# First projections of the recurrence in another order: query thirds ahead of the sample's third of the forget gate

## The chip, the cores and the metric

The kernel runs on one core of one Trainium2 chip, as one launch. The metric is the device time of that core in microseconds (us). The kernel before was timed in 3 runs: median 1388.84 us, lowest 1388.37, highest 1389.0.

## What is computed

One inference step of a two-layer encoder for two request groups that share weights: a prompt of 1024 tokens and a sample of 32 tokens. Layer 0 is sparse grouped-query attention; layer 1 is a gated linear recurrence (8 heads, keys and values of 128). Between them stands a residual add and an RMS norm. The change lies at the border of the two layers. The part of the reference that matters:

```
h = h + attn_out                                   # layer 0 ends
hn = rmsnorm(h, norm_w[1])                         # layer 1 begins
p = hn @ w_in                                      # 1024 -> 4096 columns
q, fp, vi, z = split_cols(p, [REC_KW, REC_KW, REC_WIDTH, REC_WIDTH])
f = lb + (1.0 - lb) * jax.nn.sigmoid(fp)           # forget gate
q = jax.nn.silu(q)
g = jnp.log(f)
k = 1.0 - f
# per head: b = cumsum(g); decays exp(b_t - b_s); scores, outputs and states from q, k, v and the decays
```

## The kernel before, in words

**Tokens and tiles.** The 1056 tokens are 9 tiles: tiles 0 to 7 are the prompt's, 128 tokens each, tile 8 (`SAMPLE`) holds the sample's 32. Layer 1 wants the normed tokens with the model dimension on the partitions. So TensorE (PE) turns each tile with 8 transposes in two groups of four (`turn`, L1310 to L1320), and VectorE (DVE) splits the turned values into a high and a low part (`hn_hi`, `hn_lo`; `split_normed`, L177 and L180), two groups a tile. The sample's normed rows can be made only after its own output product, its residual add, its squares (ScalarE, ACT) and its mean and root (GpSimd, POOL).

**Projections.** Each head has 4 weight tiles of 1024 x 128 (forget, query, value, gate, in this order), and each is multiplied with all tokens in three thirds of 352 tokens (`project(i)`, i = 3 x weight tile + third; 24 matmuls each: L190). Third 0 needs tiles 0 to 2, third 1 tiles 0 to 5, third 2 all of them, the sample's too. A result lies in one of four PSUM banks, taken in turn: bank `(i + 2) % 4`. ACT reads it (`read_projection`, L1731) with Sigmoid for the forget gate, Silu for query and gate, a copy for the value, and the read frees the bank for the projection four places later. The semaphores count places: `acc_ready` the finished projections, `acc_read` the read ones. The first four places wait instead for the last reads of the attention's output product (`out_read`).

**Order around the change.** Every engine's order is written out by hand. PE: output products of tiles 0 to 8, with the turn of tile t - 1 behind the products of tile t; then `project(0)`, `project(1)`, turn of the sample, `project(2)`, and in the loop over heads `project(3)` onwards, with transposes and small products (L1654 k_T, L1658 v_T, L1663 state, L1671 pairs) between. DVE: the splits of tile 7 and of the sample, then the recurrence's constants, whose first instruction (L1891) raises `lb_done`. ACT: the sample's squares, then a wait for `lb_done` and a small Exp (L1742), then the reads of the forget gate's three thirds, the logarithm (L1754), the cast of the next weight tile (L1406) and the query's three thirds. A change of function from Sigmoid to Silu, Ln or Exp puts an ACT_TABLE_LOAD ahead.

**Behind the forget gate.** When all three thirds are read, DVE makes the forget gate (`forget`, L1967 and L1970), after the logarithm a scan (L1926), the differences for the decays (L1929 to L1946: 16 instructions, and between those from L1929 on no semaphore wait), and, when ACT has taken their exponentials (`decay`, L1760), products with the query (`scale_queries`, L1951 to L1963). POOL makes the products with the key (L1839 to L1852), and between them the low parts of the weights (L1413). Then DVE does the next head's `forget` and `carry` (L1984 to L1992), for which PE waits with its pairs.

**Weights.** SyncE (SP) loads a weight tile into one of 3 slots when the last third of the tile that held the slot is done (L1596).

```
            project(0)
            project(1)
            S["turn_sample"](pe)
            project(2)
```

Of the kernel before, what the change touches and what calls it, by code (L numbers as in the profile page):

```python
# [31 lines left out]
SAMPLE = NT - 1  # L32
CW = T // 3
# [151 lines left out]
def product(pe, out, left, right):  # L185

    passes = [(l, r) for k in range(KT) for l, r in ((left[0](k), right[0](k)), (left[0](k), right[1](k)),
                                                     (left[1](k), right[0](k)))]
    for n, (l, r) in enumerate(passes):
        last = pe.matmul(out, l, r, start=n == 0, stop=n == len(passes) - 1)  # L190
    return last
# [1051 lines left out]
def attention_out(nc, S):  # L1243

    io, sem, ps, wide = S["io"], S["sem"], S["ps"], S["wide"]
    stats, half, gT, ident = S["stats"], S["half"], S["gT"], S["ident"]
    w_lo_done, x_in = S["wo_lo_done"], [sem("x2_in0"), sem("x2_in1")]
    g_hi_done, g_lo_done, shifted = sem("g_hi_done"), sem("g_lo_done"), sem("sample_rows")
    added = sem("sample_added")
    out_ready, h_ready, squares_ready = sem("out_ready"), sem("h_ready"), sem("sq1")  # L1250
    mean_ready, rstd_ready, hn_scaled = sem("mean1"), sem("rstd1"), sem("hn_scaled")
    tr_ready, hi_done, lo_done, stored = sem("tr1"), sem("hn_hi1"), sem("hn_lo1"), [sem("h_stored0"), sem("h_stored1")]
# [12 lines left out]
    if True:  # L1265
# [28 lines left out]
        def tensor(pe):  # L1294
            for t in range(NT):
                pe.wait_ge(g_lo_done, t + 1)
                for n in range(2):
                    u = 2 * t + n
                    if u == 0:
                        continue  # L1300
                    if u >= 4:
                        pe.wait_ge(h_ready, u - 3)
                    if u == 1:
                        pe.wait_ge(w_lo_done, 4)
                    output_product(pe, S, (g_hi, g_lo), (w_hi, w_lo), t, n,
                                   range(KT - 1 if u == 2 else 0, KT)).then_inc(out_ready, 1)
                if t >= 1:
                    turn(pe, t - 1)

        def turn(pe, t):  # L1310

            r = rows(t)
            pe.wait_ge(hn_scaled, t + 1)
            for g in range(2):
                if t >= 1:
                    pe.wait_ge(lo_done, 2 * (t - 1) + g + 1)
                for k in range(4):
                    kk = 4 * g + k
                    last = pe.transpose(wide[:, g, k * P:k * P + r], hn[0:r, kk * P:kk * P + P], ident[0:r, 0:r])
                last.then_inc(tr_ready, 1)  # L1320
# [68 lines left out]
                norm_stats_pool(pool, stats, half, t, squares_ready, t + 1, mean_ready, rstd_ready, rows(t))  # L1389

    S["early_out"], S["split_gated_hi"], S["split_gated_lo"] = early_out, split_gated_hi, split_gated_lo
    S["turn_sample"], S["hn_lo1"], S["out_read"], S["sample_read"] = lambda pe: turn(pe, SAMPLE), lo_done, h_ready, shifted
    S["h_stored"], S["out_done"] = stored, out_ready
    return dict(sync=sync, tensor=tensor, scalar=scalar, gpsimd=gpsimd, vector=vector)

# [21 lines left out]
def recurrence(nc, S):  # L1417
# [11 lines left out]
    SLOTS = REC_SLOTS  # L1429


    PER_HEAD = 12
# [35 lines left out]
    by_act = [u[0] in ("k_T", "v_T", "out") for u in products]  # L1468
    n_act = [sum(by_act[:i]) for i in range(len(products) + 1)]
    n_dve = [i - n for i, n in enumerate(n_act)]  # L1470

    def states_done(head):

# [117 lines left out]
    if True:  # L1591
        def sync(sp):
            def load(c):
                if c >= SLOTS:
                    sp.wait_ge(acc_ready, 3 * (c - SLOTS + 1))
                sp.dma_start(raw[:, c % SLOTS], rec_weights(io, c)).then_inc(raw_in[c % SLOTS], 16)  # L1596

            sp.wait_ge(S["out_done"], 2 * NT)
            sp.dma_start(wide_masks, io["level_masks"].rearrange("s l t -> s (l t)")).then_inc(const_in, 16)
            sp.dma_start(twos[:], io["twos_mask"]).then_inc(const_in, 16)  # L1600
            for c in range(SLOTS, len(REC_TILES)):
                load(c)

            def load_weights(c):
                ks, cols = weight_pieces()[c]
                sp.dma_start(S["wf_raw"][:, ks, cols], w_final[:, ks, cols]).then_inc(wf_in[c], 16)

            def load_gated(t):
                sp.dma_start(S["gT"][:, 0:STORED, span(t)],
                             g_dram[0:STORED, :, span(t)].rearrange("h p t -> p h t")).then_inc(g_in[t], 16)  # L1610

            sp.wait_ge(acc_ready, RH * PER_HEAD)
            load_weights(0)
            load_weights(1)
            sp.wait_ge(g_stored, 16 * STORED)
            load_gated(0)
            load_gated(1)
            load_weights(2)
            load_weights(3)
            for t in range(2, NT):  # L1620
                load_gated(FINAL_ORDER[t])

        def tensor(pe):
            def project(i):
                c, part = divmod(i, 3)
                if i >= 4:
                    pe.wait_ge(acc_read, i - 3)
                else:
                    pe.wait_ge(S["out_read"], 2 * SAMPLE - 1 + i)
                if i < 3:  # L1630
                    pe.wait_ge(S["hn_lo1"], 2 * (((part + 1) * CW + P - 1) // P))
                if part == 0:
                    pe.wait_ge(lo_done, c + 1)
                last = product(pe, ps[(i + 2) % 4][:, 0:CW], [lambda n, x=x: x[:, c % SLOTS, n, :] for x in w],
                               [lambda n, x=x: x[:, n, part * CW:(part + 1) * CW] for x in hn])
                last.then_inc(acc_ready, 1)

# [48 lines left out]
                last.then_inc(product_ready, 1)  # L1686

            project(0)
            project(1)
            S["turn_sample"](pe)  # L1690
            project(2)
            for p in range(RH):
                u = p * PER_HEAD
                for j in range(3, 9):
                    project(u + j)
                project(u + 9)
                for g in range(3):
                    multiply("v_T", p, g)
                for j in range(10, 12):
                    project(u + j)  # L1700
                if p:
                    for g in range(3):
                        multiply("out_T", p - 1, g)
                if p + 1 < RH:
                    project(u + PER_HEAD)
                for g in range(3):
                    multiply("k_T", p, g)
                if p + 1 < RH:
                    for j in range(1, 3):
                        project(u + PER_HEAD + j)  # L1710
                for g in range(3):
                    multiply("state", p, g)
                for level in [LEVELS] + list(range(LEVELS)):
                    for g in pair_groups(level):
                        multiply("pairs", p, g, level)
                for g in range(3):
                    multiply("out", p, g)
# [6 lines left out]
        def scalar(act):  # L1724
            def read_projection(i):
                head, j = divmod(i, PER_HEAD)
                slot, (part, third) = head % 2, divmod(j, 3)
                function = (ACT.Sigmoid, ACT.Silu, ACT.Copy, ACT.Silu)[part]
                dst = (k[:, slot], q[:, slot], vT, zT[:, slot])[part]
                act.wait_ge(acc_ready, i + 1)  # L1730
                act.activation(dst[:, third * CW:(third + 1) * CW], ps[(i + 2) % 4][:, 0:CW], function).then_inc(acc_read, 1)  # L1731

            def read_product(kind, head, g, dst):
                i = at[kind, head, g, None]
# [8 lines left out]
            def forget_gate(head):  # L1743
                if head >= 2:
                    act.wait_ge(product_ready, at["pairs", head - 2, 1, LEVELS] + 1)
                    act.wait_ge(k_scaled, 8 * (head - 1))
                read_projection(head * PER_HEAD)
                if head:
                    for g in range(3):
                        read_product("k_T", head - 1, g, kbT)  # L1750
                for j in range(1, 3):
                    read_projection(head * PER_HEAD + j)
                act.wait_ge(g_ready, head + 1)
                act.activation(logs[:], logs[:], ACT.Ln).then_inc(log_done, 1)  # L1754
# [18 lines left out]
            for p in range(RH):  # L1773
                u = p * PER_HEAD
                if p >= 2:
                    act.wait_ge(q_scaled, 8 * (p - 1))
                for j in range(3, 6):
                    read_projection(u + j)
                split(4 * p + 1 + SLOTS)
                for j in range(5):  # L1780
# [98 lines left out]
        def vector(dve):  # L1879
# [83 lines left out]
                dve.tensor_tensor(x, x, level_view(levels[:, LEVELS], 1)[:, :, 1, :], ALU.mult).then_inc(q_scaled, 1)  # L1963

            def forget(head):
                dve.wait_ge(acc_read, head * PER_HEAD + 3)
                dve.tensor_scalar(k[:, head % 2, :], k[:, head % 2, :], bound[:, 5, head:head + 1], bound[:, 4, head:head + 1], ALU.mult,  # L1967
                                  ALU.add).then_inc(f_ready, 1)
                dve.wait_ge(f_ready, head + 1)
                dve.tensor_scalar(logs[:], k[:, head % 2, :], G_FLOOR, 1.0, ALU.max, ALU.min).then_inc(g_ready, 1)  # L1970
# [256 lines left out]
```

## Time and profile before

| | |
|---|---|
| median of 3 runs | 1388.84 us |
| the profiled execution | 1389.89 us, its span 1388.1 us |
| granted TensorE clock | 0.998 of full speed |
| PE busy | 1349.7 us, 97% of the span |
| DVE, ACT, POOL busy | 901.5, 644.4, 677.5 us |

The span runs from the first to the last instruction; the execution's own time is 1.8 us longer. The border of the layers lies at about 707 us of the span. In the rows below a time is the start from the beginning of the span, then the duration; brackets hold the idle time of the engine before the instruction and what ended it. A PE row `128x352` is one of the 24 matmuls of a projection. Merged rows (x3, x8) run from the first start to the last end. `PE bank L190 x192` in the chain of waits is a stretch in which PE itself is the last thing waited for.

### The profile page before, as it was taken

How to read it: one execution, taken by the hardware profiler on the slowest of the kernel's cores; microseconds unless marked ns; L12 is line 12 of the kernel's file. 1: busy time of each engine (PE TensorE's matmuls, PEld its weight loads, DVE VectorE, ACT ScalarE, POOL GpSimd, SP SyncE). 2: the span in 40 equal slices, each digit the busy share in tenths (PEclk: the TensorE clock that was granted, in tenths of full speed). 3: DMA queues.
4: the chain of work that ended last, by engine and by line, in shares of the span. 5: the costliest groups of instructions: out<-in, count | busy, mean ns of one | idle time of the engine just before them, and what ended most of it. 6: DMA issues, size and time to landing. Idle time of an engine off the chain costs nothing.

```text
span 1388.1 us, 21204 instructions
## 1 busy us (share of the span) xinstructions
PE 1349.7 (97%) x8092; PEld 1207.2 (87%) x8092; DVE 901.5 (65%) x1669; ACT 644.4 (46%) x1155; POOL 677.5 (49%) x469
## 2 busy tenths in 40 slices
PE   6999999999998999999999999999999999999998
PEld 6999999999995555468889999999999999999786
DVE  4355556998897865435569484949495858587342
ACT  5455553988756565521135352525253434444121
POOL 2454443846466777720027382828383747464100
PEclk9999999999999999999999999999999999999999
DMA  7211111233225100002231010111111111107222
GB/s 247 83 37 31 32 31 31 78 84 95 69 62 182 31 16 4 32 28 94 81 93 48 17 52 32 41 43 37 47 37 47 37 47 37 47 7 230 85 80 91
DMA packets 101875, 86.80 MB, mean 63 GB/s; under 512 B 6640, under 2 KB 90480, under 8 KB 101776
## 3 DMA queue, kind: packets, MB, share of 16 engines
q1 hardware_dynamic: 100144, 80.63, 19.3%
q0 software_dynamic: 1632, 4.82, 0.9%
q8 instruction: 66, 1.08, 0.3%
q14 instruction: 33, 0.27, 0.1%
HBM read 65.46 MB, written 19.97 MB: 62 GB/s over the span
## 4 chain that ended last, share of the span: by engine, by line
PE 87%; DVE 7%; issue 2%; POOL 2%; ACT 1%; DMA 0%; SPq 0%; DVEq 0%; POOLq 0%; ACTq 0%
PE bank L190 45%; PE wide L1671 7%; PE bank L1568 7%; PE bank L241 6%; PE bank L1109 4%; PE wide L1080 4%; PE wide L720 4%; PE bank L1093 2%; PE wide L454 1%; PE wide L1678 1%; DVE states L1992 1%; PE wide L1681 1%; PE wide L241 1%; POOL probs L1054 1%; DVE o_rec L2036 1%
## 5 line engine op out<-in xcount | busy, mean ns | idle before, releaser
L190 PE MATMUL bank<-hn_hi,rw_hi 128*128 128x352 f32 x768 | 250.5, 326 | 1.6 <-DVE hn_lo L180 1.6
L190 PE MATMUL bank<-hn_hi,rw_lo 128*128 128x352 f32 x768 | 246.7, 321 | 0.0
L190 PE MATMUL bank<-hn_lo,rw_hi 128*128 128x352 f32 x768 | 246.4, 321 | 0.0
L190 PE MATMUL bank<-hn_hi,w_hi 128*128 128x352 f32 x648 | 209.9, 324 | 0.0
L190 PE MATMUL bank<-hn_hi,w_lo 128*128 128x352 f32 x648 | 208.0, 321 | 0.0
L190 PE MATMUL bank<-hn_lo,w_hi 128*128 128x352 f32 x648 | 207.8, 321 | 0.0
L1054 POOL TENSOR_SCALAR probs<-probs,low 128x128 f32<-128x128 f32 (+8 forms) x72 | 131.2, 1828 | 57.1 <-DVE low L1201 56.9
L190 PEld LDWEIGHTS bank<-hn_hi,rw_hi 128*128 128x128 f32 x768 | 144.1, 188 | 3.5 <-issue 3.0
L190 PEld LDWEIGHTS bank<-hn_lo,rw_hi 128*128 128x128 f32 x768 | 144.6, 188 | 0.0
L190 PEld LDWEIGHTS bank<-hn_hi,rw_lo 128*128 128x128 f32 x768 | 144.2, 188 | 0.0
L817 POOL TENSOR_TENSOR swapped<-swapped,sin 128x352 f32<-128x352 f32 x57 | 54.9, 963 | 144.9 <-ACT swapped L759 102.2
L190 PEld LDWEIGHTS bank<-hn_lo,w_hi 128*128 128x128 f32 x648 | 121.9, 188 | 0.1
L190 PEld LDWEIGHTS bank<-hn_hi,w_hi 128*128 128x128 f32 x648 | 121.6, 188 | 0.3
L190 PEld LDWEIGHTS bank<-hn_hi,w_lo 128*128 128x128 f32 x648 | 121.5, 187 | 0.0
L889 DVE TENSOR_SCALAR_CACHE_REDUCE marks<-score,bits 128x384 bf16<-128x384 f32 (+5 forms) x157 | 117.1, 805 | 1.1
L1413 POOL TENSOR_TENSOR rw_lo<-rw_raw,rw_hi 128x1024 fp32r<-128x1024 f32 x32 | 94.2, 2945 | 29.9 <-ACT rw_hi L1406 29.7
L254 POOL TENSOR_SCALAR stats<-stats 128x1 f32<-128x1 f32 (+1 forms) x26 | 6.3, 243 | 196.8 <-ACT junk L1381 96.0
L1671 PE MATMUL wide<-levels 128*128 128x128 f32 (+1 forms) x832 | 98.0, 273 | 1.2 <-DVE last_state L1992 1.1
L1671 PEld LDWEIGHTS wide<-levels 128*128 128x128 f32 (+1 forms) x832 | 92.5, 185 | 6.7 <-issue 1.9
L1217 ACT ACTIVATE probs<-probs,low 128x128 f32<-128x128 f32 (+8 forms) x72 | 55.5, 771 | 73.8 <-DVE low L1175 73.5
L1866 POOL TENSOR_TENSOR o_squares<-o_rec 128x1024 f32<-128x1024 f32 (+1 forms) x16 | 36.7, 2314 | 108.5 <-ACT o_rec L1739 108.5
L1846 POOL TENSOR_TENSOR levels<-levels,k_rec 128x528 f32<-128x528 f32 (+1 forms) x48 | 88.7, 1873 | 1.2 <-ACT levels L1760 1.2
(265 smaller groups left out, 3050.2 us busy)
## 6 DMA issues: line engine op xcount, KB each, us to landing
rw_raw<-in_rec_w_in SPq DMA_DIRECT2D x32, 512.0 KB, 4.1
w_raw<-in_att_w_in SPq DMA_DIRECT2D x27, 512.0 KB, 4.0
xin<-in_x_prompt SPq DMA_DIRECT2D x8, 512.0 KB, 4.5
wo_raw<-in_att_w_out SPq DMA_DIRECT2D x4, 1024.0 KB, 8.5
x_again<-in_x_prompt SPq DMA_DIRECT2D x8, 512.0 KB, 4.2
residual<-h_rows SPq DMA_DIRECT2D x8, 512.0 KB, 2.9
wf_raw<-in_rec_w_out SPq DMA_DIRECT2D x4, 1024.0 KB, 8.8
h_again<-residual SPq DMA_DIRECT2D x8, 512.0 KB, 4.2
```

The lines of the kernel that those rows point to most:

```text
L190: last = pe.matmul(out, l, r, start=n == 0, stop=n == len(passes) - 1)
L241: last = pe.matmul(out_bank(S, t, n), g_parts[x][:, t % 2, k, :], w_parts[y][n][:, k, :], start=k == 0 and (x, y) == kinds[0], stop=k == K ...
L720: last = pe.matmul(bank[0:rows(t), 0:size], of_queries[x], of_keys[y], start=(x, y) == (0, 0), stop=x == 1)
L889: step(dve.tensor_scalar(marks[0:r, i % 2, 0:keys(t)], tile(i, t), bound, 0.0, op, ALU.add, accum_out=counts[0:r, first + i:first + i + 1]))
L1054: pool.tensor_scalar(probs[0:r, i % RING, 0:n], probs[0:r, i % RING, 0:n], low[0:r, 2, i:i + 1], None, ALU.mult).then_inc(probs_ready, 1)
L1080: last = pe.matmul(logits[0:rows(t), i % 2, a:e], queries(group)[:, i % GROUP, 0:rows(t)], src[:, h // GROUP, a:e], start=True, stop=True)
L1109: last = pe.matmul(ps[2 + g % 2][:, 0:4 * r].rearrange("p (g q) -> p g q", g=4), src[:, kv * HD:(kv + 1) * HD], pT[0:kr, g % 2, j, :, 0:r] ...
L1217: act.activation(probs[0:r, i % RING, 0:n], probs[0:r, i % RING, 0:n], ACT.Exp, scale=-1.0, bias=low[0:r, 0, i:i + 1], accum_out=low[0:r, ...
L1413: pool.tensor_tensor(S["rw_lo"][:, slot], S["rw_raw"][:, slot], S["rw_hi"][:, slot].bitcast(F32), ALU.subtract).then_inc(S["rec_lo_done"], 1)
L1568: last = pe.matmul(ps[(2 * t + n) % 4][:], x[t % 2][:, k, :], w_n[y][:, k, :], start=k == 0 and x is f_hi and y == 0, stop=k == RH - 1 and ...
L1671: last = pe.matmul(out[:, 0:r], left, right, start=True, stop=True)
L1846: pool.tensor_tensor(x, x, level_view(k[:, slot], m)[:, :, 0, :], ALU.mult).then_inc(k_scaled, 1)
```

## The change

PE's order at the border is another. The turn of tile 7, which stood behind the output products, comes after `project(0)`. Behind it come `project(1)`, `project(3)` and `project(4)` (the query's thirds 0 and 1), then the turn of the sample, and then `project(2)`, the forget gate's last third. `turn_of(i)` gives the place of each projection in the new order (2 to place 4, 3 to place 2, 4 to place 3); bank, `acc_ready` and `acc_read` go by it. ACT reads in the new order, DVE's first `forget` waits for place 4, and SP's load of weight tile 3 does too. No instruction of PE, DVE, POOL or SP is added or taken away.

```diff
@@ attention_out, tensor @@
-                if t >= 1:
+                if 1 <= t < SAMPLE:
                     turn(pe, t - 1)
@@ recurrence @@
+    def turn_of(i):
+
+        return {2: 4, 3: 2, 4: 3}.get(i, i)
@@ sync, load @@
-                    sp.wait_ge(acc_ready, 3 * (c - SLOTS + 1))
+                    sp.wait_ge(acc_ready, turn_of(3 * (c - SLOTS) + 2) + 1)
@@ tensor, project @@
-                if i >= 4:
-                    pe.wait_ge(acc_read, i - 3)
+                n = turn_of(i)
+                if n >= 4:
+                    pe.wait_ge(acc_read, n - 3)
                 else:
-                    pe.wait_ge(S["out_read"], 2 * SAMPLE - 1 + i)
+                    pe.wait_ge(S["out_read"], 2 * SAMPLE - 1 + n)
...
-                last = product(pe, ps[(i + 2) % 4][:, 0:CW], [lambda n, x=x: x[:, c % SLOTS, n, :] for x in w],
+                last = product(pe, ps[(n + 2) % 4][:, 0:CW], [lambda n, x=x: x[:, c % SLOTS, n, :] for x in w],
@@ tensor @@
             project(0)
-            project(1)
-            S["turn_sample"](pe)
+            S["turn_rows"](pe, SAMPLE - 1)
+            for i in (1, 3, 4):
+                project(i)
+            S["turn_rows"](pe, SAMPLE)
             project(2)
             for p in range(RH):
                 u = p * PER_HEAD
-                for j in range(3, 9):
+                for j in range(3 if p else 5, 9):
                     project(u + j)
@@ scalar, read_projection @@
-                act.wait_ge(acc_ready, i + 1)
-                act.activation(dst[:, third * CW:(third + 1) * CW], ps[(i + 2) % 4][:, 0:CW], function).then_inc(acc_read, 1)
+                n = turn_of(i)
+                act.wait_ge(acc_ready, n + 1)
+                act.activation(dst[:, third * CW:(third + 1) * CW], ps[(n + 2) % 4][:, 0:CW], function).then_inc(acc_read, 1)
@@ scalar, forget_gate @@
-                for j in range(1, 3):
+                for j in range(1, 3) if head else (1, 3, 4, 2):
                     read_projection(head * PER_HEAD + j)
@@ scalar, loop over heads @@
-                for j in range(3, 6):
+                for j in range(3 if p else 5, 6):
                     read_projection(u + j)
@@ vector, forget @@
-                dve.wait_ge(acc_read, head * PER_HEAD + 3)
+                dve.wait_ge(acc_read, turn_of(head * PER_HEAD + 2) + 1)
```

PE around the turn of the sample, before (bank3 is `project(1)`, L1319 the sample's eight transposes, bank0 `project(2)`; the brackets name the semaphores waited for, `hn_lo1` is the split of a turned tile):

```order
L190 MATMUL bank3<-hn_hi_53,rw_lo_61 128x352
L1319 MATMUL wide<-ident_49,hn_rows_114 128x32 [waits hn_lo1,hn_scaled]
L1319 MATMUL wide<-ident_49,hn_rows_114 128x32 x3
L1319 MATMUL wide<-ident_49,hn_rows_114 128x32 [waits hn_lo1]
L1319 MATMUL wide<-ident_49,hn_rows_114 128x32 x3
L190 MATMUL bank0<-hn_hi_53,rw_hi_62 128x352 [waits hn_lo1,h_ready]
```

The same place now (bank1 is `project(4)`, bank2 is `project(2)`):

```order
L190 MATMUL bank1<-hn_hi_53,rw_lo_61 128x352
L1319 MATMUL wide<-ident_49,hn_rows_114 128x32 [waits hn_lo1,hn_scaled]
L1319 MATMUL wide<-ident_49,hn_rows_114 128x32 x3
L1319 MATMUL wide<-ident_49,hn_rows_114 128x32 [waits hn_lo1]
L1319 MATMUL wide<-ident_49,hn_rows_114 128x32 x3
L190 MATMUL bank2<-hn_hi_53,rw_hi_62 128x352 [waits hn_lo1,racc_read]
```

The turn stands two projections later; `project(2)` follows it directly, as before, but at place 4, so that it writes the bank that `project(0)` used and waits for a read by ACT (`racc_read`) where it waited for a read of the attention's product (`h_ready`).

ACT from the small Exp (L1742) to the first cast of a weight tile, before:

```order
L1742 ACTIVATE bound_134<-bound_134 128x8 [waits lb_done]
L1731 ACT_TABLE_LOAD
L1731 ACTIVATE k_rec_117<-bank2 128x352 [waits racc_ready]
L1731 ACTIVATE k_rec_117<-bank3 128x352 [waits racc_ready]
L1731 ACTIVATE k_rec_117<-bank0 128x352 [waits racc_ready]
L1754 ACT_TABLE_LOAD
L1754 ACTIVATE log_f_118<-log_f_118 128x1056 [waits g_ready]
L1406 CAST rw_hi_62<-rw_raw_60 128x1024 [waits rec_raw_in0]
```

The same stretch now, with the line numbers of the changed kernel (L1750 is the small Exp, L1739 the reads of projections):

```order
L1750 ACTIVATE bound_134<-bound_134 128x8 [waits lb_done]
L1739 ACT_TABLE_LOAD
L1739 ACTIVATE k_rec_117<-bank2 128x352 [waits racc_ready]
L1739 ACTIVATE k_rec_117<-bank3 128x352 [waits racc_ready]
L1739 ACT_TABLE_LOAD
L1739 ACTIVATE q_rec_116<-bank0 128x352 [waits racc_ready]
L1739 ACTIVATE q_rec_116<-bank1 128x352 [waits racc_ready]
L1739 ACT_TABLE_LOAD
L1739 ACTIVATE k_rec_117<-bank2 128x352 [waits racc_ready]
L1762 ACT_TABLE_LOAD
L1762 ACTIVATE log_f_118<-log_f_118 128x1056 [waits g_ready]
```

Two of the query's reads stand between the second and the third read of the forget gate, and two table loads more.

## Rows read from the trace of the kernel before

**Rows 1.** The page: the chain that ended last, by engine

```profile
PE 87%; DVE 7%; issue 2%; POOL 2%; ACT 1%; DMA 0%; SPq 0%; DVEq 0%; POOLq 0%; ACTq 0%
```

**Rows 2.** Timeline of PE at the border of the layers

```profile
706.73 0.60 PE L1319 MATMUL wide<-ident,hn_rows 128*128 128x128 f32 x4
708.03 0.66 PE L1319 MATMUL wide<-ident,hn_rows 128*128 128x128 f32 x4 [0.71 <-DVE hn_lo L180]
708.45 0.41 PE L190 MATMUL bank<-hn_hi,rw_hi 128*128 128x352 f32 x1
...
716.25 0.43 PE L1319 MATMUL wide<-ident,hn_rows 32*128 32x32 f32 x4
717.38 0.43 PE L1319 MATMUL wide<-ident,hn_rows 32*128 32x32 f32 x4 [0.69 <-DVE hn_lo L180]
719.38 0.40 PE L190 MATMUL bank<-hn_hi,rw_hi 128*128 128x352 f32 x1 [1.58 <-DVE hn_lo L180]
```

**Rows 3.** Chain of waits, 614 to 860 us: start, us, what

```profile
698.57 0.87 PE wide L1319 x8
...
719.38 30.76 PE bank L190 x192
750.14 0.98 PE wide L1658 x9
```

**Rows 4.** Timeline of DVE: the sample's split, then the recurrence's first instruction

```profile
717.24 0.28 DVE L177 TENSOR_TENSOR hn_hi<-wide,columns 128x128 fp32r<-128x128 f32 x1
...
719.15 0.16 DVE L1891 TENSOR_TENSOR bound<-columns 128x8 f32<-128x8 f32 x1
```

**Rows 5.** Timeline of ACT behind them

```profile
719.34 0.21 ACT L1742 ACTIVATE bound<-bound 128x8 f32<-128x8 f32 x1 [7.26 <-DVE bound L1891]
719.57 1.28 ACT L1731 ACT_TABLE_LOAD   x1
720.87 0.82 ACT L1731 ACTIVATE k_rec<-bank 128x352 f32<-128x352 f32 x2
723.47 0.47 ACT L1731 ACTIVATE k_rec<-bank 128x352 f32<-128x352 f32 x1 [1.79 <-PE bank L190]
...
739.10 1.05 ACT L1406 CAST rw_hi<-rw_raw 128x1024 fp32r<-128x1024 f32 x1 [3.72 <-DMA rw_raw<-in_rec_w_in]
...
746.30 1.15 ACT L1731 ACTIVATE v_columns<-bank 128x352 f32<-128x352 f32 x3
```

**Rows 6.** Timeline of DVE and POOL where both work on SBUF tensors

```profile
689.48 0.76 DVE L1359 TENSOR_SCALAR hn_rows<-h_rows,stats 128x1024 f32<-128x1024 f32 x1 [2.19 <-POOL stats L257]
...
701.49 2.97 DVE L1359 TENSOR_SCALAR hn_rows<-h_rows,stats 128x1024 f32<-128x1024 f32 x1 [2.18 <-POOL stats L257]
701.50 7.54 POOL L1413 TENSOR_TENSOR rw_lo<-rw_raw,rw_hi 128x1024 fp32r<-128x1024 f32 x3
...
737.56 0.70 DVE L1942 TENSOR_TENSOR levels<-log_decay 128x528 f32<-128x528 f32 x1
...
740.25 4.00 POOL L1413 TENSOR_TENSOR rw_lo<-rw_raw,rw_hi 128x1024 fp32r<-128x1024 f32 x1 [7.36 <-ACT rw_hi L1406]
...
741.27 0.70 DVE L1946 TENSOR_TENSOR levels<-log_decay 128x528 f32<-128x528 f32 x1
...
747.72 11.60 DVE L1958 TENSOR_TENSOR levels<-levels,q_rec 128x512 f32<-128x512 f32 x6
760.89 1.85 POOL L1852 TENSOR_TENSOR k_rec<-k_rec,levels 128x528 f32<-128x528 f32 x1
764.10 2.40 POOL L1413 TENSOR_TENSOR rw_lo<-rw_raw,rw_hi 128x1024 fp32r<-128x1024 f32 x1 [1.35 <-ACT rw_hi L1406]
771.84 0.83 DVE L1967 TENSOR_SCALAR k_rec<-k_rec,bound 128x1056 f32<-128x1056 f32 x1 [10.52 <-ACT k_rec L1731]
```

**Rows 7.** Timeline of PE: pairs behind the states

```profile
776.78 0.91 PE L1671 MATMUL wide<-levels 128*128 128x128 f32 x6 [0.16 <-DVE last_state L1992]
```

**Rows 8.** Windows: busy us of PE, PEld, DVE, ACT, POOL, granted clock, DMA

```profile
3.00:10.00 7.00, 1.94 (x8) 1.57 (x8) 1.29 (x1) 1.92 (x3) 0.74 (x2) 1.00 1.03 312
```

More of the change, by code:

```diff
@@ L1391, in attention_out @@
     S["early_out"], S["split_gated_hi"], S["split_gated_lo"] = early_out, split_gated_hi, split_gated_lo
-    S["turn_sample"], S["hn_lo1"], S["out_read"], S["sample_read"] = lambda pe: turn(pe, SAMPLE), lo_done, h_ready, shifted
+    S["turn_rows"], S["hn_lo1"], S["out_read"], S["sample_read"] = turn, lo_done, h_ready, shifted
     S["h_stored"], S["out_done"] = stored, out_ready
```

## The prediction, made before the changed kernel was run

> **What bounds the kernel now.** I read the chain that ended last first: 87% of it is TensorE (PE) [rows 1], so what counts is where PE stands idle and what wakes it. The timeline of PE at the border of the layers has three such places, all ended by VectorE's split of a turned tile: 0.71 us inside the turn of tile 7, 0.69 us inside the sample's turn and 1.58 us ahead of `project(2)`, together 2.98 us [rows 2]. From there the chain is PE for 30.76 us without a break [rows 3]. So the most that a new order can win is about 3 us of 1389, 0.2%. The reader is to see two more things. ACT reads nothing of the recurrence before DVE's L1891, behind the sample's split: it stood idle 7.26 us until then [rows 5]. And DVE and POOL hinder each other on SBUF tensors [rows 6].
>
> **What the change does to PE, step by step.** The output product ends at 706.73 [rows 2]; all inputs of `project(0)` are ready (its tiles 0 to 2 long ago, its weights with the first of three low parts, 701.50 + 7.54 / 3 = 704.0 [rows 6]). Two projections took 716.25 - 708.45 = 7.80 us, one 3.90 [rows 2], in a row 30.76 / 8 = 3.85 [rows 3]. So: `project(0)` 706.73 to 710.63; turn of tile 7, 0.87 [rows 3], its inputs ready, to 711.5; `project(1)`, `(3)`, `(4)` to 723.05. The 0.71 and the 0.69 go: the split that each turn waits for is ready long before. DVE's side keeps its times: the sample's normed rows wait for the turn of tile 7, now done at 711.5, and for POOL's root behind the sample's squares, which the change doesn't touch and which comes later than that; so the split of tile 7 ends as before, when the sample's hn_hi began, 717.24 [rows 4].
>
> Then the sample's turn, 0.43 a group [rows 2]: the first group starts at 723.1, is done at 723.6, the second at 724.0. `project(2)` stands directly behind, so the split of the sample is as uncovered as before: from the first hn_hi to L1891 it took 719.15 - 717.24 = 1.91 [rows 4]. That puts L1891 at 725.5. The old wait alone would release PE about there: 1.6 us idle.
>
> **The added wait.** `project(2)` now writes the bank of `project(0)`, and needs its first read by ACT. ACT is in order and behind `lb_done`: L1742 starts 0.19 after L1891's start, the first read 720.87 - 719.34 = 1.53 after that (small Exp and table load), and takes 0.41 to 0.47 [rows 4, 5]. 725.5 + 0.19 + 1.53 + 0.45 = 727.7, and PE starts about 0.14 later, as behind a split [rows 2, 4]: 727.85. PE is idle from 724.0 to 727.85, 3.85 us. Against 2.98 before this is **+0.87 us** at the start of `project(5)`, by which the same five projections are done in both orders. On ACT everything is queued behind that wait, but of it only this read is wanted by PE. The two added table loads (1.28 each [rows 5]) and two query reads take 1.28 + 0.9 + 1.28 = 3.5 us from 728.1 on: ACT is ready again at 731.6, before `project(2)` ends, so they cost nothing. Without that cover they would cost up to 2.6.
>
> A rule speaks against this size. The Trainium skill (ScalarE: Activation LUTs, What ACT_TABLE_LOAD costs) says that each switch to another set costs a drain of some 1.38 us beside the 1.28 of the load. By it the added wait would be 1.4 us longer, the estimate from the page +2.3 in place of +0.87; the trace has 0.02 us between load and first read, so the sum leaves it out.
>
> **What is late next.** The forget gate's last third is done 4.06 us after its start (719.38 to its read at 723.47 less 0.03), so at 731.9; its read moves from 723.47 to 731.93, by 8.46 us [rows 2, 5]. DVE's `forget`, logarithm, scan and differences all move by this, while PE moves by 0.87. Who waits for them?
>
> - The weight tile 3: its load moves by 8.46 too, its low part is done near 741, `project(9)` wants it near 747. Nothing.
> - ACT's exponentials: before, ACT began them when the cast of 739.10 was through; that cast waits for a load behind `project(5)` and moves by 0.87 only. The differences came one every 0.62 us, two a level, the last starting at 741.27 [rows 6]; now it starts at 749.7, and of the five exponentials ahead of the value reads at 746.30 + 0.87 [rows 5] the tightest finds its difference about 0.9 us early. Nothing, if DVE's run stays undisturbed. Between these reads and the v_T transposes (750.14 [rows 3]) there are 2.7 us more.
> - DVE and POOL after it. POOL's low part issued at 740.25 took 4.00 against 2.40 alone: it got in only when DVE's run of differences had ended at 741.97 [rows 6]. From there to 762.74 (760.89 + 1.85) the two took turns with no gap; DVE's six products took 11.60, 1.93 each, where a difference of the same size takes (741.27 - 737.56) / 6 = 0.62. Now that run ends at 750.43, and the whole packed stretch moves by 8.46: POOL is through at 771.2, DVE somewhat earlier. Before, DVE had 10.52 us of idle time behind it, until 771.84 [rows 6], and that cover shrinks to about 3 us. It holds for DVE itself, not for POOL: the next low part (L1413), which stood alone at 764.10 for 2.40, now begins at 771.2 and lasts to 773.6. DVE's `forget` of the next head is due at 771.84 + 0.87 = 772.7. It is a TENSOR_SCALAR from SBUF to SBUF like the one at 701.49, which took 2.97 against POOL's low part (the tile before, at 689.48, took 0.76) [rows 6]. So it waits until 773.6: **+0.9 us**. Bounds: 0 (POOL is through early, or DVE comes first) to 2.40 (the low part starts just ahead of it); I take 0.9 as the two rows have it. Behind `forget` stand the carries, and PE's pairs at 776.78 waited for these [rows 7], so it counts in full.
>
> Later heads are unchanged; PE is the chain there and a shift is kept.
>
> **Sum.** +0.87 + 0.9 = +1.8 us. On the profiled execution's 1389.89 that makes 1391.7; that execution is 1.05 above the median of the runs, 1388.84, from which I state the time: **1390.6 us**. Bounds of the parts: the PE gap +0.5 to +1.3 (latencies of 0.1 to 0.2 at four hand-overs), the collision 0 to 2.4.
>
> **Rivals.**
>
> *The forecast* (chance 0.48): 1390.6, its own range 1389.6 to 1392.4.
>
> *No collision* (0.27): POOL's stretch gets shorter since all its inputs are now ready, or the later waits swallow a part. Then only the PE gap stays: +0.4 to +0.9, 1389.5. For it: cover of 3 us on DVE. Against: from 741.97 to 762.74 one of the two always worked, so ready inputs make nothing shorter.
>
> *POOL gets in between the differences* (0.14). In place of the run, DVE gives way after each difference. POOL then puts its low part (2.4), its first product (about 2.4) and one level's product (about 1.2) ahead of the difference that ACT's fifth exponential needs: ready at 745.4 + 6.0 = 751.4, exponential to 752.4, three reads of 0.38 (1.15 / 3 [rows 5]) to 753.5, where PE wants to turn the values at 750.14 + 0.87 = 751.0: +2.5. The later levels repeat it ahead of the k_T transposes, about +2.2. With 0.87 that is +5.6: 1394.4. It decides from the point where a POOL instruction waits during the differences; before, only one came so late (740.25). Against it: exactly that one was held until the run's end [rows 6].
>
> The Trainium skill (SBUF — State Buffer, Who interferes with whom) says that whoever issues first holds the shared pair of ports for that whole instruction and the other blocks. Taken as one instruction at a time it is this rival, since each new difference would be the later comer; the row of 740.25, 4.00 us, differs, and for single instructions the rows agree with the page.
>
> *It wins* (0.05): the added wait isn't there, because ACT has read `project(0)` before; PE is then idle 1.6 in place of 2.98, -1.3, 1387.5. For it: the three old waits do shrink. Against: ACT's 7.26 us of idle time ended by L1891 [rows 5], and ACT's order is unchanged there.
>
> *The clock falls* (0.06) in the one gap of 3.85 us, or something not seen: one projection at half clock costs 3.9 more, 1394.5. Against: between 3 and 10 us PE was busy 1.94 of 7 and the granted clock stayed 1.00, full speed (2.4 GHz) [rows 8].
>
> **Range and chances.** A measurement of this kernel can tell 0.2%, 2.8 us, from no change. Faster than 1386.1 needs nearly all idle time gone: 0.02. Slower than 1391.6 takes in the rival of the differences and the clock (0.2) and the upper end of the forecast's collision (0.07 of its 0.48): 0.26 after rounding. The rest, 0.72, is no change. The range 1388.5 to 1393.4 holds the forecast, its bounds and the case without collision, and leaves out the gain and most of the two dear rivals.
>
> **What would show it.** The PE timeline: no idle time inside either turn, and one gap of 3 to 4 us ahead of `project(2)`, ended by ACT's read of k_rec, with two table loads more on ACT. DVE's scan near 736, its differences ending near 750, the POOL low part issued near 741 taking about 11 us. DVE's `forget` of head 1 near 772.7 taking 1.5 to 2 in place of 0.83. PE at the pairs that stood at 776.78 now near 778.5. I am wrong if the gap is ended by DVE's split, if the v_T transposes start later than 751.5, or if the `forget` is not lengthened.

## The result, and the profile after

| | us | runs |
|---|---|---|
| before | 1388.92 (1388.37 to 1389.65) | 4 |
| changed | 1395.56 (1394.96 to 1396.34) | 4 |

The ratio is 1.0048, 95% interval 1.003 to 1.0065: the change costs 6.6 us. I had forecast +1.8 us, 1390.6, with a range that ended at 1393.4. A slower kernel had been given a chance of 0.26; the size and the likeliest case were wrong.

The profiled execution of the changed kernel took 1395.57 us, span 1393.7. PE's timeline at the border, as in [rows 2] (start, duration, instruction, idle time before and what ended it):

```profile
709.43 1.04 PE L1319 MATMUL wide<-ident,hn_rows 128*128 128x128 f32 x8
...
721.93 0.68 PE L1319 MATMUL wide<-ident,hn_rows 32*128 32x32 f32 x8
726.56 0.66 PE L190 MATMUL bank<-hn_hi,rw_hi 128*128 128x352 f32 x1 [3.94 <-ACT k_rec L1739]
```

Both turns now run without a break, and one gap of 3.94 us stands ahead of `project(2)`, ended by ACT's read of the bank. That part came as forecast (3.85). The chain of waits of the changed kernel, as in [rows 3], shows what did not:

```profile
705.75 3.84 PE bank L190 x24
709.59 0.88 PE wide L1319 x8
710.47 11.53 PE bank L190 x72
...
726.56 5.67 PE bank L190 x24
...
746.17 2.89 DVE levels L1950
749.06 1.72 DVE levels L1949
750.78 1.70 DVE levels L1950
752.49 0.02 issue
752.51 1.08 ACT levels L1768
753.59 1.07 ACT v_columns L1739 x3
754.66 0.04 issue
754.71 2.18 PE wide L1663 x9
756.89 13.31 PE bank L190 x72
...
784.30 12.26 PE wide L1676 x104
```

Before, the chain was PE for 30.76 us from `project(2)` on. Now `project(2)` takes 5.67 us where the one at 705.75 took 3.84, and at the v_T transposes the chain leaves PE for DVE's differences and ACT's exponential and value reads. PE's waits have the length of that hole, and the windows (us, busy us of PE, PEld, DVE, ACT, POOL, granted clock, DMA) show the clock:

```profile
PE bank L190 <- ACT k_rec L1739: 3.9, 1, 3.9
PE wide L1663 <- ACT v_columns L1739: 3.4, 1, 3.4
```

```profile
725.00:730.00 5.00, 3.44 (x12) 3.45 (x13) 2.01 (x8) 4.94 (x7) 0.00 (x0) 0.66 0.00 0
...
755.00:760.00 5.00, 5.00 (x21) 4.94 (x20) 5.00 (x3) 2.54 (x3) 4.85 (x4) 0.50 0.00 0
```

0.50 is 1.2 of 2.4 GHz; the 0.66 of the first window is a mean of both levels. From 726.6 to 729.9 alone it was 0.50. The clock stood at the lower level right behind each of the two gaps.

**Where the time went.** Count from the end of the last output product, in the chain of waits, to the first pairs behind the states. Before, the product's row starts at 699.45 and takes 7.46 us, so it ends at 706.91; now it ends at 705.75. The stretch took 776.78 - 706.91 = 69.87 us before and 784.30 - 705.75 = 78.55 now, +8.7. Idle time: 3.94 + 3.4 against 2.98, +4.4. Half clock: `project(2)` 5.67 - 3.84 = +1.8; v_T 2.18 - 0.98 = +1.2; three projections 13.31 against 3 x 3.85 = 11.55, +1.8. That is +9.2; the 0.5 that is left over stands in no row by itself, and I put it down to turns that no longer stop and restart. Outside this stretch the spans of the two profiled executions differ by -3.1 us (5.6 us in all). The border came 1.16 us sooner, behind the same instructions. The kernel before had its own stretch at half clock in the final product, 1.53 us. The change touches neither place, so I count neither as its work; whether the order has a say in where the clock falls there is not shown (last section). The other 0.4 us are spread over the rest. The chain of the kernel before there, and its window:

```profile
1293.88 82.29 PE bank L1568 x350
```

```profile
1293.00:1298.00 5.00, 4.12 (x11) 3.30 (x12) 1.27 (x4) 0.50 (x2) 0.00 (x0) 0.66 0.00 0
```

The same stretch after:

```profile
1301.10 80.76 PE bank L1572 x350
```

### The profile page after: what moved, and what is told of

Read it like the earlier page. It is cut to its first block, busy times and chain, and to the rows that moved or that the text cites. A ratio compares the mean times of both kernels' runs of the same rounds, so it can differ in the third digit from the quotient of the medians.

```text
span 1393.7 us, 21206 instructions
## 1 busy us (share of the span) xinstructions
PE 1351.9 (97%) x8092; PEld 1209.8 (87%) x8092; DVE 908.3 (65%) x1669; ACT 647.7 (46%) x1157; POOL 676.7 (49%) x469
## 4 chain that ended last, share of the span: by engine, by line
PE 86%; DVE 8%; issue 2%; POOL 2%; ACT 2%; DMA 0%; DVEq 0%; POOLq 0%; ACTq 0%
PE bank L190 44%; PE wide L1676 7%; PE bank L1572 7%; PE bank L241 6%; PE bank L1109 4%; PE wide L1080 4%; PE wide L720 4%; PE bank L1093 2%; PE wide L454 1%; PE wide L1683 1%; DVE states L2000 1%; PE wide L1686 1%; PE wide L241 1%; PE bank L469 1%; DVE o_rec L2044 1%
```

## Why the v_T transposes waited

DVE's and POOL's timelines of the changed kernel, to lay beside [rows 6]:

```profile
741.97 2.39 DVE L1939 TENSOR_TENSOR k_to_end<-log_decay 128x32 f32<-128x32 f32 x1
...
745.50 0.68 DVE L1949 TENSOR_TENSOR levels<-log_decay 128x512 f32<-128x512 f32 x1
746.10 2.96 DVE L1950 TENSOR_TENSOR levels<-log_decay 128x512 f32<-128x512 f32 x1
748.99 1.80 DVE L1949 TENSOR_TENSOR levels<-log_decay 128x528 f32<-128x528 f32 x1
```

```profile
741.70 2.62 POOL L1413 TENSOR_TENSOR rw_lo<-rw_raw,rw_hi 128x1024 fp32r<-128x1024 f32 x1
745.63 2.88 POOL L1847 TENSOR_TENSOR k_to_end<-k_to_end,k_rec 128x1056 f32<-128x1056 f32 x1 [1.31 <-ACT k_to_end L1768]
748.47 3.44 POOL L1854 TENSOR_TENSOR levels<-levels,k_rec 128x512 f32<-128x512 f32 x2
```

Each POOL instruction got in at the next boundary between two of DVE's, and the DVE instruction behind it stretched by what was left of it (2.96 in place of 0.68). Up to the sixth difference of the levels, for which ACT's fifth exponential waits, this happened four times: 2.39 in place of 0.18, 2.96 in place of 0.68, 1.80 and 1.77 in place of 0.70 each, 6.7 us in all. My theory from here on: **A**, the gap ahead of `project(2)` is ACT's late read, held by `lb_done` (the semaphore that DVE's first instruction of the recurrence raises); **B**, the wait at v_T comes from POOL's work between DVE's differences, which were moved into POOL's busy time by the late forget gate; **D**, the half clock comes with the gaps. The rivals: DVE is too late for ACT even undisturbed; the clock falls there anyway; something else in the new order costs.

## The experiments

Each was timed beside the kernel before on the same chip; ratios are to it.

### x1: the constant first

The changed kernel with DVE's first instruction of the recurrence ahead of the sample's split.

```diff
+            S["lb_first"](dve)          # bound = columns - columns, raises lb_done
             transposed(NT - 1)
```

> The changed kernel, with DVE's instruction that raises lb_done put ahead of the split of the sample instead of behind it, so that ACT can read project(0) some 6 us earlier. Theory A (the gap of 3.94 us ahead of project(2) is made by ACT's late read of the bank, and the half clock of project(2) comes with that gap): the gap shrinks to the split's own 1.8 to 1.9 us and is ended by DVE hn_lo, project(2) takes 3.85 in place of 5.67; the wait of 3.4 us at the v_T transposes stays, since DVE's chain and PE both follow project(2). Time about 1395.6 - 2.0 - 1.8 = 1391.8 us. Rival (the clock falls there whatever the gap's length): gap shrinks, project(2) still 5.6, 1393.6 us. Rival (the gap has another cause): 1395.6 us.

Measured 1392.63 us, ratio 1.0034 (1.0022 to 1.0046). PE's waits:

```profile
PE wide L1670 <- ACT v_columns L1746: 3.4, 1, 3.4
...
PE bank L190 <- DVE hn_lo L180: 1.9, 1, 1.9
```

The gap fell to 1.9 us and is ended by the split; `project(2)` took 4.07 us. The wait at v_T stayed to the tenth. So A holds, and a gap of 1.9 brought no half clock here, one of 3.9 did. Behind v_T the half clock cost less than in the changed kernel, at the same wait: v_T 2.18 and the three projections 11.96, together 1.6 us in place of 3.0. The time lies 0.8 above the forecast for A and 1.0 below that of its rival; the profile decides between them.

### x2: POOL after the differences

```diff
+                if head == 0:
+                    pool.wait_ge(diff_ready, 9)
                 split(4 * head + 1 + SLOTS)
```

> The changed kernel, but in head 0 POOL waits until all nine differences are made before its next low part of the weights and its key products, so that it can't take the port between them. Theory B (the v_T wait comes from POOL's instructions getting in between DVE's differences, so that ACT's exponentials are late and hold the value reads): the 3.4 us wait at v_T goes, and with it the half clock behind it (2.95 us); DVE's differences take 8.7 us in a row; DVE's forget of head 1 may collide with a POOL low part, 0 to 1 us. Time about 1395.6 - 6.3 + 0.5 = 1389.8 us. Rival (DVE's chain is just 8.5 us later and too late for ACT even undisturbed): v_T wait still 2 to 3 us, 1395 us.

Measured 1390.16 us, ratio 1.0015 (1.0006 to 1.0024). The chain of waits:

```profile
727.11 24.74 PE bank L190 x144
751.84 0.98 PE wide L1663 x9
752.82 11.56 PE bank L190 x72
...
773.54 1.79 DVE k_rec L1977
```

POOL's low part, held back by the new wait:

```profile
751.40 2.38 POOL L1413 TENSOR_TENSOR rw_lo<-rw_raw,rw_hi 128x1024 fp32r<-128x1024 f32 x1 [9.17 <-DVE levels L1956]
```

No wait at v_T (ACT's value reads start at 747.91, take 1.15 and end 2.8 us ahead of the transposes), and the second stretch at half clock is gone (11.56 for the three projections). DVE's `forget` began 27.07 us behind the border, as in the changed kernel (733.37 - 706.30, 732.82 - 705.75), so its lateness alone did nothing: B holds. And here the collision that I had forecast for the changed kernel does appear: the `forget` of head 1 takes 1.79 in place of 0.83, +0.96 against my 0.9. In the changed kernel PE was so late that POOL was through before it.

### x3: the value reads earlier

```diff
-                for j in range(5):
+                for j in range(5 if p else 3):
                     decay(p, j)
...
                 for j in range(6, 9):
                     read_projection(u + j)
+                for j in range(5 if p else 3, 5):
+                    decay(p, j)
```

> The changed kernel, but in head 0 ACT reads the three value thirds behind its third exponential instead of its fifth. Theory B (ACT's order hands DVE's lateness to PE, at whichever read comes behind the late exponentials): the wait at v_T goes, but a new one of about 4 us stands at the k_T transposes, which need ACT's copies of v behind the ninth exponential. Time 1393 to 1395.6 us. Rival (the v_T wait is the whole loss, and behind it there is slack): 1395.6 - 6.3 = 1389.3 us.

Measured 1396.32 us, ratio 1.006 (1.0043 to 1.0077). PE's wait:

```profile
PE wide L1659 <- ACT v_rec L1747: 3.6, 1, 3.6
```

The wait left v_T and came back at k_T with 3.6 us. This reordering of ACT only moves it.

### x4: the turn of tile 7 alone

The kernel before, with `project(0)` ahead of the turn of tile 7 and nothing else.

> The kernel before, with one part of the change alone: the turn of tile 7 moved behind project(0); project(0), (1), (2), (3) in the old order. Theory C (DVE's chain from the sample's sum to its split sets when project(2) can start, so PE's saved 0.71 us is idled away ahead of the sample's turn): project(2) starts within 0.1 us of 719.4 after the same start, time as before, 1388.9 us. Rival (each idle place on PE counts): 1388.9 - 0.7 = 1388.2 us.

Measured 1388.05 us, ratio 1.0002 (0.9993 to 1.0012): no difference, and too coarse to part the theory from its rival, which lie 0.7 us apart. The profile does. PE waited 0.30 us ahead of the sample's turn, 1.26 inside it and 1.38 ahead of `project(2)`, 2.94 in place of 2.98:

```profile
712.32 0.41 PE L1319 MATMUL wide<-ident,hn_rows 32*128 32x32 f32 x4 [0.30 <-DVE hn_lo L180]
713.99 0.63 PE L1319 MATMUL wide<-ident,hn_rows 32*128 32x32 f32 x4 [1.26 <-DVE hn_lo L180]
716.00 0.63 PE L190 MATMUL bank<-hn_hi,rw_hi 128*128 128x352 f32 x1 [1.38 <-DVE hn_lo L180]
```

`project(2)` started 12.5 us behind the last output product, as before. The chain through the sample's sum, its norm and the two splits sets when `project(2)` can start.

### x10: both repairs, the order as changed

x1's and x2's edits together.

> The changed order of PE as it is, with both repairs: lb_done raised ahead of the sample's split (as in x1) and POOL held back until the nine differences of head 0 are made (as in x2). Theory A and B together (the late read of the bank and the wait at the v_T transposes, each with its stretch at half clock, are the whole loss): PE has one gap of 1.9 us ahead of project(2) in place of 2.98 before, no wait at v_T, DVE's forget of head 1 about 1 us late by POOL's low part; 1.1 us won, 1.0 us lost: 1388.1 us against 1388.6. Rival (something else in the new order costs too): 1390 us or more.

Measured 1388.81 us, ratio 1.0006 (0.9997 to 1.0015). In the profile the stretch from border to pairs takes 775.65 - 706.16 = 69.49 us, 0.4 less than before, and PE works through the v_T transposes without a wait:

```profile
724.96 23.13 PE bank L190 x144
748.09 0.98 PE wide L1670 x9
```

The two mechanisms are the whole loss within what can be measured.

### x5, x7, x8: where the order could go

x5 turns the sample one projection earlier, so that `project(4)` covers the split and ACT's read; x7 adds POOL's wait; x8 is a smaller version with only `project(3)` ahead of `project(2)`, behind the turn.

```diff
-            for i in (1, 3, 4):                  # changed kernel
-                project(i)
-            S["turn_rows"](pe, SAMPLE)
+            for i in (1, 3):                     # x5, x7 (both with lb_done first)
+                project(i)
+            S["turn_rows"](pe, SAMPLE)
+            project(4)
             project(2)
```

> The changed kernel with the turn of the sample one projection earlier (order project(0), turn 7, (1), (3), turn of the sample, (4), (2)) and lb_done ahead of the sample's split; POOL free. Now the split and ACT's read lie beside project(4), so PE has no gap ahead of project(2) (3 us won against before), but DVE's chain is still two query projections later than before as PE counts it: the wait of 3.4 us at v_T stays, with 1 to 3 us at half clock. Time 1388.6 - 3.0 + 3.4 + 2 = 1391 us. Rival (with no gap ahead of it the v_T wait shrinks too): 1387 us.

> As x5, and POOL held back until the nine differences of head 0 are made. Both mechanisms gone and the gap covered: no idle time of PE from project(0) to the k_T transposes; 2.98 us won, about 1 us lost where DVE's forget of head 1 meets POOL's low part: 1388.6 - 2.0 = 1386.6 us. Rival (idle time only moves to the next wait): 1388.6 us.

> Only one of the query's thirds goes ahead, and it stands behind the sample's turn: order project(0), turn 7, (1), turn of the sample, (3), (2). project(2) writes the bank that the attention's product freed, so no read by ACT is waited for; project(3) covers the split. PE waits only for the split of tile 7 inside the sample's turn, about 1.4 us in place of 2.98. DVE's chain is one projection later in PE's count, 3.85 us, and the differences end near 744, so POOL meets only their last third. Theory B: no wait at v_T or under 1 us, 1388.6 - 1.5 = 1387.1 us. Rival (any lateness of the forget gate comes back at v_T in full): 1389 to 1391 us.

| | us | ratio, 95% interval |
|---|---|---|
| x5 | 1389.34 | 1.0005 (0.9996 to 1.0014) |
| x7 | 1384.90 | 0.9978 (0.9968 to 0.9988) |
| x8 | 1386.72 | 0.9992 (0.9983 to 1.0001) |

x5 has no gap at the border and still 3.3 us at v_T, so what it wins it gives back; its rival falls:

```profile
PE wide L1670 <- ACT v_columns L1747: 3.3, 1, 3.3
```

Its time lies 1.7 under the forecast. The half clock explains little of that (2 us forecast, 1.8 in its profile); its profile also has no half clock in the final product, 1.5 us that the kernel before lost there, but one profile can't show this for the median. x7's chain of waits is PE alone from the sample's turn to v_T:

```profile
718.14 0.61 PE wide L1319 x8
718.75 27.01 PE bank L190 x168
745.76 0.98 PE wide L1670 x9
```

x7 is faster than the kernel before by 3.1 us (1.7 to 4.4). That is 1.7 more than forecast; its profile too has no half clock in the final product (80.81 us). x8 has no wait at v_T, and its differences ran undisturbed, which agrees with B; its gain of about 1 us can't be told from none. It shows something else (below).

### x11: the gap filled

```diff
             S["turn_rows"](pe, SAMPLE)
+            for n in range(20):
+                pe.matmul(wide[:, 2, 0:CW], w[0][:, 0, n % KT, :], hn[0][:, n % KT, 0:CW], start=True, stop=True)
             project(2)
```

> The kernel of x2 (changed order, POOL held back until the differences are made) with 20 matmuls of 128x352 between the sample's turn and project(2), about 3.2 us in the gap of 3.94 us, into a PSUM tile that nobody reads; their results are thrown away. Theory D (project(2) runs at half clock because PE stood idle ahead of it): project(2) takes 3.85 in place of 5.4 to 5.7 us and starts at the same time, x2's 1390.2 - 1.7 = 1388.5 us, although PE does more. Rival (the clock falls at that point in any case, or the dummies push project(2) back): 1390.2 to 1391 us.

Measured 1389.39 us, ratio 1.0009 (0.9998 to 1.0021). As a time this is inconclusive beside x2's 1.0015. In its profile the chain reads

```profile
726.48 23.16 PE bank L190 x144
...
777.19 13.88 PE wide L1676 x104
```

The six projections behind the gap take 23.16 us, in x2 24.74: with PE at work the clock did not fall there. It fell at the pairs in this execution (13.88 against 12.26), behind smaller waits that were there in every run. So filling the gap took the half clock from that place, but I can't show that it saves the time.

### x12: the low part behind the forget

x7 with POOL's low part of weight tile 6 behind its key step of head 1.

```diff
+                if head:
                     split(4 * head + 3 + SLOTS)
...
                     keep(head + 1)
+                    if head == 0:
+                        split(3 + SLOTS)
```

> The kernel of x7 (1384.9 us) with POOL's low part of weight tile 6 in head 0 behind its key step of head 1, so that it can't stand in front of DVE's forget of head 1. Theory E (the forget at 767.46, 1.70 us, waited 0.87 us for the port that POOL's low part held, and PE's pairs waited for it in full): forget takes 0.83 again, PE's pairs 0.9 us earlier, 1384.0 us. Rival (the wait only moves to the next DVE instruction, or later waits swallow it): 1384.9 us.

Measured 1385.20 us, ratio 0.9974 (0.9965 to 0.9984). The chain of waits:

```profile
767.41 0.84 DVE k_rec L1986
```

The `forget` is back to its own time and the pairs start at 772.35, in x7 at 773.27: the 0.9 us is there. The profiled execution lost it again at half clock in the final product (82.19 us, in x7 80.81), and the ratios of x7 and x12 overlap, so in the total it is not shown. It is the best version by its ratio, 3.6 us under the kernel before.

## Why the prediction was wrong, step by step

- *The idle places of PE and the added wait.* Right. 3.85 us forecast, 3.94 measured, ended by ACT's read; both turns without a break. x1 shows that the late `lb_done` makes 2.0 of it.
- *The table loads.* Right that they cost nothing: ACT had both added loads and four reads done and then waited 1.96 us for `project(2)`. The first read again followed its load with 0.02 us between, as in the kernel before. The drain that the Trainium skill (ScalarE: Activation LUTs, What ACT_TABLE_LOAD costs) adds to a load does not show in that row either.
- *"Nothing, if DVE's run stays undisturbed"*, the step that let the value reads through with 0.9 us to spare. This is the step that failed. I took one row, POOL's low part that was held for 1.6 us until DVE's run ended [rows 6], for a rule. In the changed kernel POOL's low part at 741.70 took 2.62 us where I had forecast about 11, POOL got in at four places before the difference that the value reads hang on was made, v_T waited 3.4 us, and the kernel paid 3.0 more at half clock behind it; x2, with POOL kept out, has neither. This was my second rival, with 0.14; it had 2.5 us at v_T and another 2.2 at k_T, and the second did not come, since PE was late enough by then. The rule on the shared pair of ports (the Trainium skill, SBUF — State Buffer, Who interferes with whom), one instruction at a time, gives the rows of the changed kernel, where I let one row overrule it; the held rows of the kernel before, x4 and x8 it does not give.
- *The clock.* Forecast with 0.06, for one gap. It fell behind both gaps and cost 4.8 us in all, more than the idle time added. The size that I had given it, 3.9 us for one gap, was too large: the gap ahead of `project(2)` cost 1.8. The row with PE busy for 1.94 of 7 us at full clock [rows 8] was taken as evidence that gaps are harmless; it was from the first microseconds of the span, and the kernel before itself fell to half clock behind a wait of 2.3 us at 1293.88, which I had not looked for since the mean of 0.998 looked like nothing.
- *The collision at the next forget.* Wrong for the changed kernel (0), right in x2 and x7 (0.96 and 0.87) where PE was on time. Of the forecast's two terms the first was right (+0.96 for 0.87), the second did not come, and the loss lay in what I had put at nothing.

## What to carry to other kernels

Moving independent work ahead of a waited-for piece hides the wait and delays everything that hangs on that piece. Follow that chain until it joins again, engine by engine and with what shares a port with it; here the far end cost more than the near end could win. A stall on a busy PE is to be priced with the half clock that may come behind it: 3.9 us idle cost 1.8 more in the changed kernel, 1.6 in x2 and 1.5 in x3; 3.3 to 3.4 us idle cost 3.0 more in the changed kernel, 1.6 in x1 and 1.8 in x5. The price is not fixed by the length of the gap.

## What the runs showed of the hardware

**Whether POOL gets in between DVE instructions is not settled by one row.** In x8 POOL's low part came during the differences and was held through the one under way and the eight behind it. First POOL's row, then DVE's:

```profile
739.50 7.75 POOL L1413 TENSOR_TENSOR rw_lo<-rw_raw,rw_hi 128x1024 fp32r<-128x1024 f32 x1 [3.62 <-ACT rw_hi L1406]
```

```profile
739.31 0.70 DVE L1950 TENSOR_TENSOR levels<-log_decay 128x528 f32<-128x528 f32 x1
...
744.88 2.40 DVE L1959 COPY decay_end<-q_from_start 128x8 f32<-128x8 f32 x1
```

7.75 us for 2.4 us of work, and DVE's next instruction with a semaphore wait, at 744.88, is the first that gave way. POOL came 0.19 us after the start of a difference here and 0.21 in the kernel before (740.25 against 740.04). In x4 it came 0.58 us after one (738.82 against 738.24), just ahead of the next, and was held too (4.23 us).

At 745.63 in the changed kernel POOL came 0.13 us after a difference and got in, with a product with the key (L1847). At 741.70 it got in with a low part, late in the long first subtraction of DVE's run (L1937, from 738.81 to 742.05). So neither the kind of POOL's instruction nor a late arrival decides by itself; whether the offset, the pair of instructions that meet or something else does is open. What is safe is not to have POOL arrive in such a run at all (x2, x7).

**Half clock comes and goes at small gaps.** Behind the wait of 2.3 us ahead of the final product the clock fell in the profiles of the kernel before, x1, x2, x8, x10, x11 and x12, and not in those of the changed kernel, x3, x4, x5 and x7, at the same wait. In x4's profile it fell behind waits of 0.30 and 1.26, before the one of 1.38 (granted clock 1.00 from 712.5 to 713.5, 0.50 from 714.5 to 715.5), and the eight projections took 33.00 us for 30.76. In x8's profile it fell behind waits of 0.29 and 1.26 (32.42 us). Behind the three waits of the kernel before, 0.71, 0.69 and 1.58, it stayed up. Single runs of the kernel before spread from 1386.15 to 1391.09 us over 30 runs, about as much as two or three such stretches of 1.5 to 1.8 us explain; that they are its cause is argued, not shown.
